# Four gate tiles of block one as joint products of high and low part, in shared pairs of PSUM banks

## What is computed

```python
def hybrid_layer(h, ...):
    u = rms_norm(h, g_mix_pre)
    (gq, gk, gv, gg, ra_f, ra_b, aq, ak, av, gate_a, gate_b) = jnp.split(u @ w_in, offsets, axis=-1)
    ...
    o_gla = rms_norm(o_f + o_b, g_gla_out).reshape(b, s, GLA_VAL)
    branch_a = (o_gla * jax.nn.silu(gg)) @ w_o_gla
    q = apply_axial_rope(rms_norm(aq, g_q_norm), cos, sin)
    k = apply_axial_rope(rms_norm(ak, g_k_norm), cos, sin)
    branch_b = gqa_attention(q, k, v) @ w_o_attn
    mixed = jax.nn.sigmoid(gate_a) * branch_a + jax.nn.sigmoid(gate_b) * branch_b
    h = h + rms_norm(mixed @ w_out, g_mix_post)
```

## Time and profile before

| | |
|---|---|
| median of 3 executions | 2306.16 us (2306.08 to 2306.39) |
| profiled execution, its own time | 2306.12 us |
| its span | 2304.3 us |
| TensorE busy | 99% of the span |
| VectorE busy | 68% |
| ScalarE busy | 57% |
| mean granted clock of TensorE | 0.999 |
| chain that ended last | PE 75%, DVE 14%, ACT 9%, issue 1% |

### The profile page before, as it was taken

How to read it: one execution, slowest core, us unless ns; L and a number is a source line. 1 busy time by engine, 2 the same in 40 slices (tenths; PEclk the granted TensorE clock), 3 DMA queues, 4 the chain that set the end, 5 groups by cost and what they waited for, 6 DMA issues and landing times.

```text
span 2304.3 us, 31105 instructions
## 1 busy us (share of the span) xinstructions
PE 2272.0 (99%) x13028; PEld 1995.5 (87%) x13028; DVE 1570.7 (68%) x1797; ACT 1322.7 (57%) x1801; POOL 42.7 (2%) x76
## 2 busy tenths in 40 slices
PE   8999999999999999999999999999999999999998
PEld 8888888888998988888898888888888898988886
DVE  6866776479766775667577766664776578666755
ACT  6675655476755654655458645554554458555544
POOL 1000000010000000010000000000100000000000
PEclk9999999999999999999999999999999999999999
DMA  7715555556245655465555455555655645455553
GB/s 224 230 61 183 188 190 195 185 181 224 92 149 181 212 191 192 165 216 188 186 184 165 128 183 190 185 191 193 195 195 182 204 153 165 147 183 181 184 192 119
DMA packets 323515, 411.92 MB, mean 179 GB/s; under 512 B 11600, under 2 KB 245456, under 8 KB 323376
## 3 DMA queue, kind: packets, MB, share of 16 engines
q1 hardware_dynamic: 318160, 394.68, 52.6%
q0 software_dynamic: 4928, 14.26, 2.0%
q10 hardware_dynamic: 288, 0.99, 0.1%
HBM read 408.85 MB, written 1.05 MB: 178 GB/s over the span
## 4 chain that ended last, share of the span: by engine, by line
PE 75%; DVE 14%; ACT 9%; issue 1%; DMA 0%; SPq 0%; DVEq 0%; ACTq 0%
PE banks L602 19%; PE banks L610 10%; PE banks L679 9%; PE banks L681 9%; PE banks L680 9%; DVE lo L1743 7%; ACT hi L1168 5%; PE banks L586 3%; PE banks L587 3%; PE banks L588 3%; DVE mg L1889 1%; PE banks L730 1%; DVE mg L1793 1%; PE banks L863 0%; PE banks L667 0%
## 5 line engine op out<-in xcount | busy, mean ns | idle before, releaser
L1743 DVE TENSOR_TENSOR lo<-raw,hi 128x2048 fp32r<-128x2048 f32 (+1 forms) x382 | 858.6, 2251 | 566.1 <-ACT hi L1168 565.7
L1168 ACT ACTIVATE hi<-raw 128x2048 fp32r<-128x2048 f32 (+1 forms) x382 | 715.3, 1876 | 221.5 <-DMA raw<-in_ffn_w_out 85.4
L602 PE MATMUL banks<-x_in,hi 128*128 128x512 f32 x2304 | 538.0, 390 | 0.7 <-issue 0.6
L602 PEld LDWEIGHTS banks<-x_in,hi 128*128 128x128 f32 x2304 | 427.5, 188 | 87.5 <-issue 1.2
L610 PEld LDWEIGHTS banks<-x_in,lo 128*128 128x128 f32 x2304 | 286.6, 192 | 6.9 <-issue 0.9
L610 PE MATMUL banks<-x_in,lo 128*128 128x256 f32 x2304 | 289.6, 283 | 0.8 <-issue 0.6
L586 PE MATMUL banks<-x_in,hi 128*128 128x256 f32 x736 | 210.5, 286 | 0.0
L588 PE MATMUL banks<-x_in,lo 128*128 128x256 f32 x736 | 208.2, 283 | 0.0
L587 PE MATMUL banks<-x_in,hi 128*128 128x256 f32 x736 | 208.2, 283 | 0.0
L679 PE MATMUL banks<-hi,x_hid 128*128 128x512 f32 x528 | 206.0, 390 | 0.0
L681 PE MATMUL banks<-hi,x_hid 128*128 128x512 f32 x528 | 205.5, 389 | 0.0
(11 more groups left out here) (338 smaller groups left out, 3102.2 us busy)
## 6 DMA issues: line engine op xcount, KB each, us to landing
raw<-in_w_in SPq DMA_DIRECT2D x108, 1024.0 KB, 5.2
raw<-in_ffn_w_in SPq DMA_DIRECT2D x88, 1024.0 KB, 5.1
raw<-in_w_ffn_in SPq DMA_DIRECT2D x44, 1024.0 KB, 5.1
raw<-in_ffn_w_out SPq DMA_DIRECT2D x40, 1024.0 KB, 5.1
raw<-in_w_ffn_out SPq DMA_DIRECT2D x20, 1024.0 KB, 5.1
raw<-in_w_o_gla SPq DMA_DIRECT2D x8, 1024.0 KB, 5.1
raw<-in_w_o_attn SPq DMA_DIRECT2D x8, 1024.0 KB, 5.2
raw<-in_w_out SPq DMA_DIRECT2D x8, 1024.0 KB, 5.1
```

What stands on the lines that cost most here:

```text
L602: mm = pe.matmul(bank[b + f], wh[:, k, f * P:(f + 1) * P], x[:, k, :, :].rearrange("p n s -> p (n s)"), start=(start and k == 0), stop=(k ...
L1168: act_fn(high, of, ACT.Copy).then_inc(hi_done.up(), 1)
L1743: tt(rest, of, parts(tile, hi)[0].bitcast(F32), ALU.subtract).then_inc(lo_done.up(), 1)
```

## The change

The four gate tiles are formed with `joint_b`. Gate tile j takes the two banks 0 and 1 for j = 0 and 2, and 2 and 3 for j = 1 and 3. ScalarE gets one copy per tile (the second half sums to the new buffer `gate_half`), VectorE one addition per tile out of PSUM ahead of the multiplication, which now reads and writes SBUF. The banks are given back by `sum_in`, the addition. The second key tile `gk[1]` goes to bank 4 instead of 2, and the pairs of the values and queries move from (3, 0), (1, 2), (3, 0) to (2, 3), (0, 1), (2, 3), in all that write or read them.

```diff
-    ... "sum_in": (33, 53), "half_ev": (33, 53),
+    ... "sum_in": (37, 53), "half_ev": (37, 53),
+        gate_half = at("gate_half", [P, 2, 512], o_f)
-        gate_bank = (1, 2, 0, 3)
+        gate_bank = (0, 2, 0, 2)
 # TensorE
-                for tile, b in ((gq[1], 0), (gk[0], 1), (gk[1], 2)):
+                for tile, b in ((gq[1], 0), (gk[0], 1), (gk[1], 4)):
-                pairs = [(3, 0), (1, 2), (3, 0), (6, 7)]
+                pairs = [(2, 3), (0, 1), (2, 3), (6, 7)]
...
-                    form_b(tile, x_in, gate_bank[j])
-                    freed[gate_bank[j]] = scaled.next()
+                    joint_b(tile, x_in, gate_bank[j])
+                    freed[gate_bank[j]] = freed[gate_bank[j] + 1] = sum_in.next()
 # ScalarE
-                values_out(v1, 1, (3, 0))
+                values_out(v1, 1, (2, 3))
-                head_roots(0, 4, (1, 2))
+                head_roots(0, 4, (0, 1))
-                head_roots(1, 4, (3, 0))
+                head_roots(1, 4, (2, 3))
...
                         warm(ACT.Silu)
                     else:
                         pump(tile.index + 2)
+                    act.wait_ge(*tile_used.at(tile.index + 1))
+                    act_fn(gate_half[:, j % 2, :].rearrange("p (f s) -> p f s", f=2), halves(gate_bank[j], 1),
+                           ACT.Copy).then_inc(half_ev.up(), 1)
                     act.wait_ge(*scaled.at(6 + j))
                     act_fn(gg[:, 2 * j:2 * j + 2, :], gg[:, 2 * j:2 * j + 2, :], ACT.Silu).then_inc(gl_ready.up(), 1)
 # VectorE
-                heads_in(kf, 1, 2, 1.0)
+                heads_in(kf, 1, 4, 1.0)
-                rope(0, 4, (1, 2))
+                rope(0, 4, (0, 1))
-                rope(1, 4, (3, 0))
+                rope(1, 4, (2, 3))
...
                 def gates_in(j):
                     tile = BY1["gg"][j]
                     pump(tile.index + (2 if j < 3 else 1))
-                    dve.wait_ge(*tile_used.at(tile.index + 1))
-                    times_root(gg[:, 2 * j:2 * j + 2, :], bank[gate_bank[j]][:], scaled)
+                    dve.wait_ge(*half_ev.next())
+                    to = gg[:, 2 * j:2 * j + 2, :]
+                    tt(to, halves(gate_bank[j], 0), gate_half[:, j % 2, :].rearrange("p (f s) -> p f s", f=2),
+                       ALU.add).then_inc(sum_in.up(), 1)
+                    dve.wait_ge(*sum_in.now())
+                    times_root(to, to.rearrange("p f s -> p (f s)"), scaled)
```

More of the change, by code:

```diff
@@ L60 @@
     "root_ready": (2, 4), "root_full": (2, 3), "root_out": (2, 3), "gate_in": (11, 22), "scaled": (9, 9),
-    "gl_ready": (4, 4), "mg_in": (8, 8), "xf_ready": (0, 0), "sum_in": (33, 53), "half_ev": (33, 53),
+    "gl_ready": (4, 4), "mg_in": (8, 8), "xf_ready": (0, 0), "sum_in": (37, 53), "half_ev": (37, 53),
 }
```

## The result

The changed kernel takes 2322.57 us (2322.03 to 2324.31 in four executions), the kernel before 2306.12 beside it: a ratio of 1.0072 (95% interval 1.0055 to 1.009). It is 16.4 us slower. The forecast was 10.1 us and a range up to 2321.5, so the direction was right and the time lay above the range. The profiled execution has a span of 2320.2 us, 15.9 more than before.

A forecast was written before the change was run, and what follows sets the result against it. The prediction took the VectorE and ScalarE chain before L1005, not TensorE, as the bound. The late release of bank 2 delays L1005 by 5.05 us per layer: 2 x 5.05 on 2306.12 gives 2316.2 us, range 2311.8 to 2321.5.

The forecast's parts named there:

- A clock that falls: After TensorE's roughly 5 us wait before the GLA scores, a slow pace might cost 1.8 to 2.6 us per layer.
- How the numbers follow: Passage giving chances to forecast and alternatives, and the range 2311.8 to 2321.5 us; slower 0.92, same 0.06, faster 0.02.
- the case without it: The forecast itself, with no clock fall behind the waits before the GLA scores: 2316.2 us, chance 0.55.
- the sum: Two layers, each 5.05 us late at L1005, on top of 2306.12: 2316.2 us, no clock loss included.
- rival 1: TensorE's clock falls in both long waits before the GLA scores: 2319.8 to 2321.4 us, chance 0.27.
- The addition step: VectorE's addition ahead of each gate multiplication delays it by 0.72 us, with bounds of 0.61 and 0.79.
- What TensorE saves: Joint gate tiles take 5.57 us, 0.19 less each, 1.5 us in the run, worth nothing because L1005 is set elsewhere.
- The small waits for the heads: TensorE waits for copied heads until about 112.1 and 118.8 us, standing ready about 0.4 earlier; hidden.
- Rival 3: Gate 3's copy comes early enough, so only four additions count: 5.8 us, 2311.9; chance 0.11 together with another alternative.
- Rival 4: VectorE's and ScalarE's additions hide, TensorE sets the end at L1005, keeping 1.5 us saved: 2304.6 us, chance 0.05.

The follow-up runs named there:

- run one: Changed kernel with 40 identity transposes, read by nothing, before the wait for bank 2 in each layer's first GLA round: 2317.02 us.
- run two: Changed kernel with gates 0 to 2 joint and gate 3 formed by form_b in bank 3, without half copy and addition: 2311.03 us.
- run three: Changed kernel with gate 3's half copy ahead of the exponentials on ScalarE and its addition ahead of the shares on VectorE: 2311.82 us.
- run six: Kernel before with ScalarE's high parts and head copies ahead of the silu, gates 0 to 2 joint, gate 3 by form_b: 2303.43 us.
- run five: Kernel before with ScalarE making one more high part and copying transposed heads ahead of the silu for gates 0 and 1: 2303.97 us.
- run seven: Changed kernel, all four gates joint, with ScalarE's high parts and head copies moved ahead of the silu for gates 0 and 1: 2309.29 us.
- run four: Kernel before with only the gate banks changed from (1, 2, 0, 3) to (1, 3, 0, 2): 2311.22 us.
- run eight: Changed kernel with ScalarE's high parts and head copies ahead of the silu, plus 14 identity transposes before the bank 2 wait: 2307.0 us.
- nine: Kernel before with gate banks (1, 3, 0, 2) and 22 identity transposes ahead of the wait for bank 2: 2309.47 us.

## Why the prediction was wrong, point by point

**The step that failed** is the choice under "A clock that falls" and in "How the numbers follow". The text there has the mechanism, finds the nearest row (16 matmuls at twice the distance behind the wait at the start) and says what it would cost. Then it gives it 0.27 and the case without it 0.55, and the sum goes without it: a term of 2.7 us a layer stood at nothing. The waits within the run spoke neither for nor against it. The longest is not 1.4 us, as the prediction has it, but 1.6, and the granted clock behind that one (1635 to 1637 us) stays at 1.00:

```profile
PE banks L643 <- DVE x_in L1762: 1.6, 1, 1.6
```

But a wait of 4.6 us is nearer to the one of 4.49 at the start than to one of 1.6, and for this one the only rows there are show the slow pace. Whether that pace at the start was the same clock no row shows: the granted clock is given as 1.00 there, before the change and after it. In each of the four executions of the changed kernel the mean granted clock was 0.996; in the profiled one of before it was 0.999. The Trainium skill (TensorE: Matmul & The Clock Gate, Part 1) says that an idle TensorE falls to 1.2 GHz; the trace agrees, at 0.50 behind the wait. I had read that rule as making the case likely and did not let it move the chance.

**The size of that term** was low as well: 1.8 to 2.6 us a layer forecast, 7.70 - 4.96 = 2.74 in the first, and by run one 5.6 us in both. The bounds came from the start of the run. The lower one, 1.8, was not open even there, since the eight matmuls between the two rows are slow as well, 1.71 us from their start to that of the 40, or 0.21 each:

```profile
7.96 1.91 PE L730 MATMUL banks<-cst,xn 128*128 128x128 f32 x8
```

There the low pace ended after 5.2 us; here it lasted from 131.2 to about 137.2, 6 us, and in the second layer from 615.5 to about 621.9, 6.4. With the measured size rival 1 would have given 2306.12 + 2 x (5.05 + 2.8) = 2321.8. The profiled execution, the fastest of the four, took 2322.03, and the median is 0.5 above it. What differs among the four is open.

**The rest of the sum held.** The scores would start at 131.25, and they started at 131.16. Without the clock the state product would follow 1.71 + 0.93 later: 133.80, 4.96 late, forecast 5.05; run one, with the clock kept up, has 5.18 and 10.8 us in all, forecast 10.1. The addition step is 0.73 (VectorE's addition at 130.41, its multiplication at 131.14; 0.72 in the earlier trace rows), and the tiles take the 5.57 forecast. What TensorE saves on them was worth nothing, as the wait for the chain takes it. The small waits for the heads came out at 0.64 and 0.60; the first ended at 111.69, 0.4 earlier than forecast, the second at 118.75, as forecast.

**The split of the 16.4 us.** Three additions in the chain: 4.9 (run two, whose median lies among the eight of ten executions with a mean granted clock of 0.999). Gate 3's copy behind the exponentials, its addition and the bank: 6.0 more (run one less run two). The clock: 5.6 (the changed kernel less run one). Rival 3, an early copy, had 2311.9 as its price; run three builds it and has 2311.82. That they agree so closely is in part luck: the median holds what the clock cost in that execution, if anything, and each interval here is some us wide.

**Rival 4**, additions hidden behind TensorE, is wrong for this order of the queues, and right for three of the tiles once ScalarE no longer waits in front of work that is ready: in run six they let the state product start 0.6 us earlier than in run five. For the fourth it is wrong even then, because of the bank (run seven).

## What to carry to other kernels

Shorter work on the busiest engine is worth nothing where a chain of other engines sets the end of the stage; look at that chain before, and count every operation that the change adds to it. A buffer that is given back by a later instruction than before is a new wait, even where no instruction is added (run four): ask of each buffer who takes it next and where the releasing instruction stands in its own queue. And a wait on TensorE has two prices, its length and the low clock behind it; where a wait of several us appears, take the second into the sum, or fill it with matmuls that nobody reads (runs one, eight and nine).

## What the runs showed of the hardware that I had not expected

- Waits much shorter than 4.6 us can be followed by the low clock too, and not each time. The wait of 1.43 us in run three had it in one layer and not in the other, 0.87 us in run two likewise. Run seven with waits of 1.6 us spread over 7 us, and over 1.1 once they were filled (run eight). The wait of 1.9 us at L931 in run three had the low clock behind it, the one of 1.6 us at L643 in the kernel before had not. What decides it, the runs do not show. In the kernel before, with 0.8 us ahead of the state product, the granted clock is 1.00 in the profiled execution, and its 22, 27 and 21 executions beside the runs spread over 1.5, 1.1 and 1.0 us.
- At half the clock these stretches do not take quite twice as long: the GLA scores went from 1.71 to 3.13 us, the transposes from 0.93 to 1.76.
- At one place (L930 in the kernel before, L931 in the others) TensorE waits for nothing that the profile shows, for 0.3 us in the kernel before, 0.9 in run six and 1.9 in run three, with the code around it unchanged. What sets it is open.
